# Expert stage: transposes and gathers as products with narrow array tiles

## The chip, the core and the metric

The kernel runs on one core of a Trainium2 chip. A core has five engines with their own instruction streams: TensorE (PE, matrix products out of SBUF into PSUM), VectorE (DVE), ScalarE (ACT), GpSimd (POOL) and SyncE (SP, which here issues the DMA transfers). The metric is the device time of one execution in microseconds. A product on PE is a weight load (LDWEIGHTS, the stationary operand) and a MATMUL that streams the moving operand past it. The array can be used whole (128 rows by 128 columns), or as column tiles of 64 or 32 columns, each with its own small product; in the profile's shapes "128*64" is a product on a tile of 128 rows and 64 columns.

## The reference

One inference step of a two-layer backbone for 128 context tokens and 128 latent tokens, 1024 channels, all in float32. Layer 0 mixes with a long convolution and RWKV-7 and has a dense SwiGLU; layer 1 mixes with gated DeltaNet and ends in a mixture of 8 experts, of which each token uses 2. The change lies in that last part:

```
def moe_swiglu(h, router, w_in, w_out):
    logits = (h @ router).astype(jnp.float32)
    top_val, top_idx = lax.top_k(logits, TOP_K)
    gates = jax.nn.softmax(top_val, -1)
    combine = jnp.einsum('blk,blke->ble', gates, jax.nn.one_hot(top_idx, N_EXP, ...))
    out = dense_swiglu(h, w_in[0], w_out[0]) * combine[..., 0:1]
    for e in range(1, N_EXP):
        out = out + dense_swiglu(h, w_in[e], w_out[e]) * combine[..., e:e + 1]
    return out
```

with `dense_swiglu(h, w_in, w_out)`: `gate, up = split(h @ w_in)`, then `(silu(gate) * up) @ w_out`, 1024 channels to 2 x 3584 and back.

## The kernel before

The work is one sequence of stages: modulation products and the even layer, the dense SwiGLU, the odd layer, the routing, and then the expert stage from line 1849 on (in the profile from 1036 us to 1915 us of the span), a final norm and the stores.

In the expert stage the 8 experts are sorted by their number of tokens and get a fixed number of slots in that order (`MAIN_CAPS`): 128 (WIDE), 64 (HALF), and then three times 96 (MID) and 64 (HALF). This stage is called the main pass; a second pass for tokens that don't fit is skipped here by a branch. For each expert, called q below, PE does:

- a gather (line 2071): it picks the expert's tokens out of `htok` by products with the 0/1 matrix `Psel`, two halves of 16 products in the code, into bank 5; ACT copies the result to `hA`;
- 7 steps of 512 hidden channels. A step is a gate product and an up product (`in_product`, line 2079), ACT and DVE make silu(gate) x up (`actb`), PE transposes that in blocks of 128x128 (line 2106) into bank 4, ACT copies it to `actT`, and PE multiplies it into the expert's output (`project`, line 2109);
- a transpose of the slot weights `Pw` (line 2141), and a scatter (line 2147) of the expert's output back to the tokens, four parts in the steps of the next expert.

The products are shaped by the slots. WIDE uses the whole array (lines 2086, 2121). HALF puts two products of 64 columns side by side (lines 2089, 2124). MID uses four tiles of 32 columns: three take 384 of the 512 weight columns (lines 2094, 2129), the fourth takes the remaining 128 for all three groups of tokens one after the other (lines 2097, 2132). Transposes, gathers and weight transposes use the whole array in every step, the scatter uses the whole width with as many rows as the expert has slots.

The order on PE in step i is written out by hand (line 2155): gate product of i, transposes of i-1, then one of: weight transposes (first step of an expert, for the expert before), scatter part (steps 1 to 4), gather half for the next expert (steps 5 and 6), then the up product of i and the output product of i-1. A transposed block is 128 columns of `actb`: there are 4 in a WIDE step, 3 in a MID step, 2 in a HALF step.

Weights come from HBM through a ring of 7 tiles of 2 MB (`load` in `sp_pass`): 3 tiles a step, 168 in the pass, one DMA each, all from SP in order. A load waits until PE has finished the product that used its slot 7 tiles before; a product waits until its tile has landed.

Of the kernel before, what the change touches and what calls it, by code (L numbers as in the profile page):

```python
# [14 lines left out]
P = 128  # L15
T = 128
# [10 lines left out]
NE = 8  # L27
# [120 lines left out]
def program(nc, A, O):  # L148
    ctx = ExitStack()
    with ctx:  # L150
# [28 lines left out]
        ps = [ctx.enter_context(nc.psum_tensor(f"bank{i}", [P, 512], F32)) for i in range(8)]  # L179
# [14 lines left out]
        def take(*shape, rows=P):  # L194

            n = 1
            for k in shape:
                n *= k
            assert floats[0] + n <= ARENA, (floats[0], n, ARENA)
            ap = arena[0:rows, floats[0]:floats[0] + n]  # L200
            floats[0] += n
            if len(shape) == 1:
                return ap
            names = "abcd"[:len(shape)]
            return ap.rearrange(f"p ({' '.join(names)}) -> p {' '.join(names)}", **{names[i]: shape[i] for i in range(len(shape))})
# [12 lines left out]
        def cc(name):  # L218
            g, o, k = CCOL[name]
            return cons[g][:, o:o + k]  # L220

        ident, ones, bones = cc("ident"), cc("ones"), cc("bones")
# [1626 lines left out]
        WIDE, MID, HALF = T, 3 * T // 4, T // 2  # L1849
# [6 lines left out]
        htok = take(NS, D)  # L1856
# [5 lines left out]
        Psel = take(NS, T)  # L1862
        Pw = take(NS, T)
# [147 lines left out]
        actb = take(2, 512)  # L2011
# [6 lines left out]
        KC = EFF // 512  # L2018
        STEPS = NE * KC
# [48 lines left out]

        def pe_pass(pe, m):

            def gather(q, half):
                c = m.caps[q]
                for j in range(4 * half, 4 * half + 4):
                    for s in range(NS):
                        mm = nc.tensor.matmul(ps[5][:, (j % 4) * T:(j % 4) * T + c], htok[:, s, j * P:(j + 1) * P], Psel[:, s, 0:c],  # L2075
                                              start=(s == 0), stop=(s == 1))
                mm.then_inc(m.gat, 1)

            def in_product(i, n, out):
                c, h = m.caps[i // KC], hA[:, (i // KC) % 2]  # L2080
                m.arrived(pe, n)
                w = m.tile(n).rearrange("p (j c) -> p j c", j=8)
                for j in range(DC):
                    start, stop = j == 0, j == DC - 1
                    if c == WIDE:
                        mm = nc.tensor.matmul(out[:], h[:, j, :], w[:, j, :], start=start, stop=stop)  # L2086
                    elif c == HALF:
                        for x in range(2):
                            mm = nc.tensor.matmul(out[HALF * x:HALF * x + HALF, 0:256], h[:, j, 0:HALF],  # L2089
                                                  w[:, j, 256 * x:256 * x + 256], start=start, stop=stop,  # L2090
                                                  tile_position=(0, HALF * x))
                    else:
                        for lo, hi in ((0, 32), (32, HALF), (HALF, MID)):
                            nc.tensor.matmul(out[lo:hi, 0:3 * P], h[:, j, lo:hi], w[:, j, 0:3 * P], start=start, stop=stop,  # L2094
                                             tile_position=(0, lo), skip_group_check=True)
                        for r in range(3):
                            mm = nc.tensor.matmul(out[MID:P, r * P:(r + 1) * P], h[:, j, 32 * r:32 * r + 32], w[:, j, 3 * P:4 * P],  # L2097
                                                  start=(start and r == 0), stop=stop, tile_position=(0, MID), skip_group_check=True)
                mm.then_inc(m.used, 1)

            def transposes(i):
                pe.wait_ge(m.act, m.base + i + 1)
                if i:
                    pe.wait_ge(m.aT, m.base + i)
                for f in range(m.width(i) // P):
                    mm = nc.tensor.transpose(ps[4][:, f * T:(f + 1) * T], actb[:, i % 2, f * P:(f + 1) * P], ident)  # L2106
                mm.then_inc(m.tr, 1)

            def project(i):
# [28 lines left out]
            def weights(q):  # L2138
                pe.wait_ge(m.Pw, m.base + q + 1)
                for s in range(NS):  # L2140
                    mm = nc.tensor.transpose(ps[5][:, s * T:(s + 1) * T], Pw[:, s, :], ident)
                mm.then_inc(m.Ct, 1)

            def scatter(q, b, bank):
                c = m.caps[q]
                for d in (2 * b, 2 * b + 1):
                    mm = nc.tensor.matmul(bank[:, (d % 2) * TT:(d % 2 + 1) * TT], ye[0:c, d * P:(d + 1) * P], Cw[0:c, :],  # L2147
                                          start=True, stop=True)
                mm.then_inc(m.sc, 1)

            pe.wait_ge(m.P, m.base + 1)
            gather(0, 0)
            pe.wait_ge(m.hA, m.base + 1)
            gather(0, 1)
            for i in range(STEPS):
                q, k = divmod(i, KC)
                if k == 0:
                    pe.wait_ge(m.hA, m.base + 2 * q + 2)
                if i >= 2:
                    pe.wait_ge(m.act, m.base + i - 1)  # L2160
                in_product(i, gate_at(i), ps[2 * (i % 2)])
                if i:
                    transposes(i - 1)
                if k == 0 and q:
                    weights(q - 1)
                if 1 <= k <= 4 and q:
                    if k == 1:
                        pe.wait_ge(m.C, m.base + q)
                        pe.wait_ge(m.ye, m.base + q)
                    else:  # L2170
                        pe.wait_ge(m.acc, m.base + 4 * (q - 1) + k - 1)
                    scatter(q - 1, k - 1, ps[5])
                if k >= 5 and q < NE - 1:
                    if k == 5:
                        pe.wait_ge(m.P, m.base + q + 2)
                        if q:
                            pe.wait_ge(m.acc, m.base + 4 * q)
                    else:
                        pe.wait_ge(m.hA, m.base + 2 * q + 3)
                    gather(q + 1, k - 5)  # L2180
                if i == STEPS - 1:
                    pe.wait_ge(m.acc, m.base + 4 * q)
                    weights(q)
                in_product(i, up_at(i), ps[2 * (i % 2) + 1])
                if i:
                    project(i - 1)
            transposes(STEPS - 1)
            project(STEPS - 1)
            pe.wait_ge(m.act, m.base + STEPS)
# [125 lines left out]
        with nc.Block() as block:  # L2315
# [25 lines left out]
            @block.tensor  # L2341
            def _(pe):
                with pe.If(more(pe) > 0):
                    pe_pass(pe, rest)
                    pe.wait_ge(rest.acc, rest.base + 4 * NE)
                pe_pass(pe, main)
                n4.pe(pe, ps[0])
# [142 lines left out]
```

## Time and profile before

| what | value |
|---|---|
| median of 3 runs | 1940.58 us (1939.35 to 1944.2) |
| the profiled execution's own time | 1933.93 us |
| its span, first to last instruction | 1932.2 us |
| PE busy | 1777.2 us (92%), 18321 MATMULs |
| granted PE clock, mean of the span | 0.962 |
| DMA queue of the weights (q1) | 489.90 MB, 61.7% of 16 engines' span |
| instruction fetch (q8) | 146 packets, 2.39 MB |

The profile gives busy time by engine, a picture of the span in slices, the chain of work that ended last (followed back from the last instruction), and groups of instructions by line. Times are in us from the start of the span. A float32 product in the code stands in the trace as two LDWEIGHTS and two MATMULs, a transpose as one of each. MATMULs overlap, so the pace of a group is its length in the chain over its count, not the mean duration of one.

### The profile page before, as it was taken

Reading aid. Unit: us, or ns where it says so; the run is one execution under the profiler, and the core shown is the slowest. Engines: PE = TensorE matmul, PEld = TensorE weight load, DVE = VectorE, ACT = ScalarE, POOL = GpSimd, SP = SyncE. Lnnn points to the kernel's source line nnn. Section 1 sums busy time; section 2 is a strip of 40 time slices with the busy share of each in tenths; the row PEclk is TensorE's granted clock in tenths of the full one; section 3 lists DMA queues with packets and bytes.
Section 4 is the critical chain, followed back from the end, with each engine's and each line's share of the span. In section 5 each row is a group of like instructions: output and inputs, shape, how many; then the busy total and the mean of one; then the engine's idle time right before and its main releaser. Section 6 shows DMA issues by size and latency. Waiting matters only on the chain. (4 is left out here: it accounts for less than half of the span.)

```text
span 1932.2 us, 40334 instructions
## 1 busy us (share of the span) xinstructions
PE 1777.2 (92%) x18321; PEld 1399.3 (72%) x18321; DVE 533.4 (28%) x1222; ACT 294.5 (15%) x638; POOL 72.3 (4%) x109
## 2 busy tenths in 40 slices
PE   6996888899999898788887999999999999999995
PEld 3884777778888687677775444579966897589853
DVE  5436667530000347266633000100000000000003
ACT  1112333110000143323211000010010001000101
POOL 0002222000000000000000000000000000000000
PEclk9998999999999899888896999999999999999998
DMA  9809542224342432000004987999999999999993
GB/s 390 332 25 428 204 177 89 99 87 174 131 174 88 180 136 88 7 13 13 13 6 186 428 338 302 419 426 426 420 421 426 426 424 421 428 425 426 408 428 166
DMA packets 37133, 492.54 MB, mean 255 GB/s; under 512 B 4380, under 2 KB 4541, under 8 KB 7453
## 3 DMA queue, kind: packets, MB, share of 16 engines
q1 hardware_dynamic: 36956, 489.90, 61.7%
q8 instruction: 146, 2.39, 0.5%
q14 instruction: 31, 0.25, 0.0%
HBM read 487.53 MB, written 2.36 MB: 254 GB/s over the span
## 5 line engine op out<-in xcount | busy, mean ns | idle before, releaser
L2097 PE MATMUL bank<-ring,arena 128*32 128x128 f32 x2016 | 227.6, 273 | 0.0
L2094 PE MATMUL bank<-ring,arena 128*32 128x384 f32 x2016 | 224.8, 487 | 1.8 <-DMA ring<-in_experts 1.8
L2097 PEld LDWEIGHTS bank<-ring,arena 128*32 128x32 f32 x2016 | 217.9, 110 | 0.0
L2089 PE MATMUL bank<-ring,arena 128*64 128x256 f32 x1792 | 204.8, 381 | 2.7 <-DMA ring<-in_experts 2.7
L2089 PEld LDWEIGHTS bank<-ring,arena 128*64 128x64 f32 x1792 | 126.2, 137 | 80.2 <-issue 22.5
L2291 DVE TENSOR_TENSOR arena<-bank,arena 128x256 f32<-128x256 f32 (+2 forms) x56 | 28.5, 508 | 545.1 <-PE bank L2097 155.1
L1374 PE MATMUL bank<-arena,ring 128*128 128x256 f32 x704 | 155.3, 382 | 4.0 <-DVE arena L321 3.8
L1374 PEld LDWEIGHTS bank<-arena,ring 128*128 128x128 f32 x704 | 133.9, 191 | 24.5 <-issue 4.1
L2247 ACT ACTIVATE arena<-bank 128x256 f32<-128x256 f32 (+2 forms) x56 | 25.3, 452 | 697.4 <-PE bank L2097 293.6
L1495 PE MATMUL bank<-arena,ring 128*128 128x256 f32 x512 | 115.6, 388 | 6.4 <-DVE arena L321 3.8
L1495 PEld LDWEIGHTS bank<-arena,ring 128*128 128x128 f32 x512 | 98.6, 194 | 24.8 <-issue 5.8
L2132 PE MATMUL bank<-ring,arena 128*32 128x128 f32 x1008 | 113.5, 273 | 0.0
L2129 PE MATMUL bank<-ring,arena 128*32 128x384 f32 x1008 | 112.1, 486 | 0.0
L2132 PEld LDWEIGHTS bank<-ring,arena 128*32 128x32 f32 x1008 | 109.8, 110 | 0.0
L2124 PE MATMUL bank<-ring,arena 128*64 128x512 f32 x448 | 101.2, 593 | 3.9 <-DMA ring<-in_experts 3.9
L2086 PE MATMUL bank<-ring,arena 128*128 128x512 f32 x224 | 98.3, 593 | 1.5 <-DMA ring<-in_experts 1.5
L2265 DVE TENSOR_TENSOR arena<-arena,bank 128x512 f32<-128x512 f32 x32 | 22.0, 688 | 274.4 <-PE bank L2147 274.4
L583 PE MATMUL bank<-arena,ring 128*128 128x256 f32 (+1 forms) x416 | 92.1, 385 | 5.0 <-DVE arena L297 5.0
L583 PEld LDWEIGHTS bank<-arena,ring 128*128 128x128 f32 (+1 forms) x416 | 80.0, 193 | 16.9 <-issue 5.2
L2094 PEld LDWEIGHTS bank<-ring,arena 128*32 128x32 f32 x2016 | 80.6, 109 | 11.7 <-issue 11.3
L2086 PEld LDWEIGHTS bank<-ring,arena 128*128 128x128 f32 x224 | 42.0, 190 | 51.9 <-issue 50.2
L1385 PE MATMUL bank<-arena,ring 128*128 128x256 f32 x352 | 77.0, 379 | 0.0
(393 smaller groups left out, 2210.2 us busy)
## 6 DMA issues: line engine op xcount, KB each, us to landing
ring<-in_experts SPq DMA_DIRECT2D x168, 2048.0 KB, 20.5
ring<-in_stream SPq DMA_DIRECT2D x61, 2048.0 KB, 11.9
xT<-in_xT SPq DMA_DIRECT2D x1, 1024.0 KB, 7.4
arena<-in_s0gd SPq DMA_DIRECT2D x4, 256.0 KB, 3.4
out_sgd<-arena SPq DMA_DIRECT2D x4, 256.0 KB, 2.5
out_y<-arena SPq DMA_DIRECT2D x4, 256.0 KB, 2.5
arena<-in_masks SPq DMA_DIRECT2D x1, 832.0 KB, 7.1
arena<-in_hfw SPq DMA_DIRECT2D x1, 544.0 KB
```

Of the source, the lines that this page charges most:

```text
L583: mm = nc.tensor.matmul(ps[m % 4][0:rows, 0:TT], tile_in(n)[:, j, f * P:f * P + rows], hT[:, j, :], start=(j == 0), stop=(j == DC - 1))
L1374: mm = nc.tensor.matmul(ps[4 + m % 4][:, half * TT:(half + 1) * TT], w[:, j, half * 256 + f:half * 256 + f + P], hT[:, j, :], start=(j == ...
L1385: mm = nc.tensor.matmul(ps[d // 2][:, (d % 2) * TT:(d % 2 + 1) * TT], tile_out(tile)[:, f % 4, d * P:(d + 1) * P], act4[:, k % 2, f % 4, : ...
L1495: mm = nc.tensor.matmul(ps[m % 4][:, 0:TT], tile_in(n)[:, j, f * P:(f + 1) * P], hT[:, j, :], start=(j == 0), stop=(j == DC - 1))
L2086: mm = nc.tensor.matmul(out[:], h[:, j, :], w[:, j, :], start=start, stop=stop)
L2089: mm = nc.tensor.matmul(out[HALF * x:HALF * x + HALF, 0:256], h[:, j, 0:HALF], w[:, j, 256 * x:256 * x + 256], start=start, stop=stop, til ...
L2094: nc.tensor.matmul(out[lo:hi, 0:3 * P], h[:, j, lo:hi], w[:, j, 0:3 * P], start=start, stop=stop, tile_position=(0, lo), skip_group_check= ...
L2097: mm = nc.tensor.matmul(out[MID:P, r * P:(r + 1) * P], h[:, j, 32 * r:32 * r + 32], w[:, j, 3 * P:4 * P], start=(start and r == 0), stop=s ...
L2124: mm = nc.tensor.matmul(ps[6][HALF * h:HALF * h + HALF, :], aT[:, f % 2, o:o + HALF], w[:, f, 512 * h:512 * h + 512], start=start, stop=st ...
L2129: nc.tensor.matmul(ps[6 + h][lo:hi, 0:3 * P], aT[:, f, lo:hi], w[:, f, o:o + 3 * P], start=start, stop=stop, tile_position=(0, lo), skip_g ...
L2132: mm = nc.tensor.matmul(ps[6 + h][MID:P, r * P:(r + 1) * P], aT[:, f, 32 * r:32 * r + 32], w[:, f, o + 3 * P:o + 4 * P], start=(start and ...
L2291: V.tensor_tensor(actb[:, i % 2, 0:n], ps[2 * (i % 2) + 1][:, 0:n], sgl[:, i % 2, 0:n], ALU.mult).then_inc(m.act, 1)
```

## The change

A helper `strands` writes one product of the code as 128/w products of w columns each, one on each column tile of the array, where w is the width of the products of the expert that PE is working on then: 128 in WIDE, 64 in HALF, 32 in MID. The two transposes (of `actb` and of `Pw`) become such products with the unit matrix `ident` as the moving operand, and the gather's products are cut the same way. WIDE is included: there a transpose becomes one whole product with `ident`. The scatter is left as it is, and so are the order of the steps, the waits and the loads.

```diff
--- before.py
+++ after.py
@@ -2068,12 +2068,21 @@
 
         def pe_pass(pe, m):
 
-            def gather(q, half):
+            STRAND = {WIDE: P, HALF: 64, MID: 32}
+
+            def strands(out, left, right, q, start=True, stop=True):
+                w = STRAND[m.caps[q]]
+                for x in range(0, P, w):
+                    mm = nc.tensor.matmul(out[x:x + w], left[:, x:x + w], right, start=start, stop=stop,
+                                          tile_position=(0, x), skip_group_check=True)
+                return mm
+
+            def gather(q, half, during):
                 c = m.caps[q]
                 for j in range(4 * half, 4 * half + 4):
                     for s in range(NS):
-                        mm = nc.tensor.matmul(ps[5][:, (j % 4) * T:(j % 4) * T + c], htok[:, s, j * P:(j + 1) * P], Psel[:, s, 0:c],
-                                              start=(s == 0), stop=(s == 1))
+                        mm = strands(ps[5][:, (j % 4) * T:(j % 4) * T + c], htok[:, s, j * P:(j + 1) * P], Psel[:, s, 0:c], during,
+                                     start=(s == 0), stop=(s == 1))
                 mm.then_inc(m.gat, 1)
 
             def in_product(i, n, out):
@@ -2103,7 +2112,7 @@
                 if i:
                     pe.wait_ge(m.aT, m.base + i)
                 for f in range(m.width(i) // P):
-                    mm = nc.tensor.transpose(ps[4][:, f * T:(f + 1) * T], actb[:, i % 2, f * P:(f + 1) * P], ident)
+                    mm = strands(ps[4][:, f * T:(f + 1) * T], actb[:, i % 2, f * P:(f + 1) * P], ident, min(i + 1, STEPS - 1) // KC)
                 mm.then_inc(m.tr, 1)
 
             def project(i):
@@ -2138,7 +2147,7 @@
             def weights(q):
                 pe.wait_ge(m.Pw, m.base + q + 1)
                 for s in range(NS):
-                    mm = nc.tensor.transpose(ps[5][:, s * T:(s + 1) * T], Pw[:, s, :], ident)
+                    mm = strands(ps[5][:, s * T:(s + 1) * T], Pw[:, s, :], ident, min(q + 1, NE - 1))
                 mm.then_inc(m.Ct, 1)
 
             def scatter(q, b, bank):
@@ -2149,9 +2158,9 @@
                 mm.then_inc(m.sc, 1)
 
             pe.wait_ge(m.P, m.base + 1)
-            gather(0, 0)
+            gather(0, 0, 0)
             pe.wait_ge(m.hA, m.base + 1)
-            gather(0, 1)
+            gather(0, 1, 0)
             for i in range(STEPS):
                 q, k = divmod(i, KC)
                 if k == 0:
@@ -2177,7 +2186,7 @@
                             pe.wait_ge(m.acc, m.base + 4 * q)
                     else:
                         pe.wait_ge(m.hA, m.base + 2 * q + 3)
-                    gather(q + 1, k - 5)
+                    gather(q + 1, k - 5, q)
                 if i == STEPS - 1:
                     pe.wait_ge(m.acc, m.base + 4 * q)
                     weights(q)
```

PE's order around the first HALF expert's first two steps, as the program issues it (a row is line, operation, out<-in, shape of the output, number in the code). Before, L2089 and L2124 are HALF products, L2121 WIDE output products, L2106 and L2141 transposes, L2147 the scatter:

```order
L2121 MATMUL bank<-ring,arena 128x512 x8
L2089 MATMUL bank<-ring,arena 64x256 x16
L2106 MATMUL bank<-con,arena 128x128 x4
L2141 MATMUL bank<-con,arena 128x128 x2
L2089 MATMUL bank<-ring,arena 64x256 x16
L2121 MATMUL bank<-ring,arena 128x512 x8
L2089 MATMUL bank<-ring,arena 64x256 x16
L2106 MATMUL bank<-con,arena 128x128 x2
L2147 MATMUL bank<-arena 128x256 x2
L2089 MATMUL bank<-ring,arena 64x256 x16
```

and of the changed kernel, where L2098, L2133 and L2130 are those products, L2156 the scatter, and L2076 the product inside `strands`:

```order
L2130 MATMUL bank<-ring,arena 128x512 x8
L2098 MATMUL bank<-ring,arena 64x256 x16
L2076 MATMUL bank<-con,arena 64x128 x12
L2098 MATMUL bank<-ring,arena 64x256 x16
L2130 MATMUL bank<-ring,arena 128x512 x8
L2098 MATMUL bank<-ring,arena 64x256 x16
L2076 MATMUL bank<-con,arena 64x128 x4
L2156 MATMUL bank<-arena 128x256 x2
L2098 MATMUL bank<-ring,arena 64x256 x16
```

The four transposes of a WIDE step and the two of the weights became 12 products of 64 columns, and the two transposes of a HALF step 4; they stand at the same place.

The same around a gather in a MID step; before, L2094 and L2097 are the MID products and L2075 is the gather:

```order
L2094 MATMUL bank<-ring,arena 32x384 x3
L2097 MATMUL bank<-ring,arena 32x128 x3
L2106 MATMUL bank<-con,arena 128x128 x3
L2075 MATMUL bank<-arena 128x64 x8
L2094 MATMUL bank<-ring,arena 32x384 x3
L2097 MATMUL bank<-ring,arena 32x128 x3
```

and after, where L2103 and L2106 are the MID products:

```order
L2103 MATMUL bank<-ring,arena 32x384 x3
L2106 MATMUL bank<-ring,arena 32x128 x3
L2076 MATMUL bank<-con,arena 32x128 x12
L2076 MATMUL bank<-arena 32x64 x32
L2103 MATMUL bank<-ring,arena 32x384 x3
L2106 MATMUL bank<-ring,arena 32x128 x3
```

Three transposes became 12 products of 32 columns, and the gather's 8 products of 128 columns became 32 of 32 columns.

## Rows read from the trace of the kernel before

**Rows 1.** Windows: length; PE, PEld, DVE, ACT, POOL busy (count); clock; DMA share; GB/s.

```profile
1050.00:1115.00 65.00, 65.00 (x162) 29.39 (x161) 2.46 (x5) 3.86 (x7) 0.00 (x0) 1.00 1.01 429
1120.00:1192.00 72.00, 72.00 (x203) 34.27 (x203) 2.58 (x5) 4.03 (x8) 0.00 (x0) 1.00 0.80 294
1207.00:1905.00 698.00, 689.77 (x8645) 535.14 (x8645) 47.99 (x100) 61.63 (x169) 0.00 (x0) 1.00 1.00 420
1390.00:1406.00 16.00, 16.00 (x238) 13.71 (x232) 0.56 (x1) 1.22 (x4) 0.00 (x0) 1.00 0.98 392
1486.00:1695.00 209.00, 206.87 (x2711) 165.85 (x2711) 14.19 (x30) 18.47 (x51) 0.00 (x0) 1.00 1.01 425
1695.00:1905.00 210.00, 204.29 (x2683) 162.71 (x2683) 13.79 (x28) 18.15 (x51) 0.00 (x0) 1.00 0.98 412
```

**Rows 2.** DMA in 1125 to 1207 us: issues, KB, median us to landing.

```profile
ring<-in_experts SPq DMA_DIRECT2D x12, 2048.0 KB, 7.7
```

**Rows 3.** DMA in 1207 to 1905 us: instruction fetch, and the tiles' issues.

```profile
q8 instruction: 68, 1.11, 0.6%
...
ring<-in_experts SPq DMA_DIRECT2D x139, 2048.0 KB, 21.7
```

**Rows 4.** Chain of waits, WIDE expert: start us, length us, what.

```profile
1068.94 0.44 PE bank L2106 x4
...
1153.54 1.73 PE bank L2075 x16
```

**Rows 5.** Chain of waits, from WIDE into the first HALF expert.

```profile
1195.49 0.59 PE bank L2106 x4
1196.08 0.22 PE bank L2141 x2
1196.30 3.60 PE bank L2089 x32
1199.90 7.06 PE bank L2121 x16
1206.97 3.60 PE bank L2089 x32
```

**Rows 6.** Chain of waits, a HALF step with a scatter, and a gather.

```profile
1242.30 3.45 PE bank L2089 x32
1245.75 0.37 PE bank L2106 x2
1246.12 0.87 PE bank L2147 x4
1246.98 3.60 PE bank L2089 x32
...
1257.85 1.76 PE bank L2075 x16
```

**Rows 7.** Chain of waits, MID: transposes with a scatter, and before a gather.

```profile
1316.96 0.48 PE bank L2106 x3
1317.44 1.06 PE bank L2147 x4
...
1785.22 0.48 PE bank L2106 x3
```

**Rows 8.** Chain of waits: loads from issue to landing, at three HALF ends.

```profile
1460.57 25.51 DMA ring<-in_experts
...
1667.58 27.56 DMA ring<-in_experts
...
1876.64 28.43 DMA ring<-in_experts
```

**Rows 9.** PE's waits, 1395 to 1500 us: line, releaser, us, times, longest.

```profile
PE bank L2094 <- DMA ring<-in_experts: 0.6, 1, 0.6
```

**Rows 10.** PE instructions by form: busy us, mean ns.

```profile
L2106 PE MATMUL bank<-con,arena 128*128 128x128 f32 x147 | 28.0, 292 | 0.0
```

**Rows 11.** Timeline of PE, modulation products: start us, length us, what.

```profile
197.90 2.61 PE L376 MATMUL bank<-ring,silc 128*32 128x128 f32 x88
```

## The prediction

> **What bounds the kernel now.** I read the windows of the expert stage first. From 1120 to 1192 us, in the WIDE expert, PE is busy all the time and the DMA engines only 0.80 of it: the ring is full, and each load waits for PE. From 1207 to 1905 us the DMA share is 1.00 at 420 GB/s [rows 1]. The DMA view says the same: a tile lands 7.7 us after its issue up to 1207 [rows 2], and 21.7 us after it from there on [rows 3], so that several loads always stand in the queue. So the stage has two parts. Up to about 1207 the end moves with PE. From there it moves with the DMA: 139 loads stand in a row, and PE is late only where the ring is full.
>
> How far PE is from the bound there: after the second HALF expert (1486 us) PE waits 0.6 us for a tile [rows 9], in the next pair of MID and HALF 209.00 - 206.87 = 2.1 us, and in the last pair 210.00 - 204.29 = 5.7 us [rows 1]. The waits grow, so PE is the faster of the two over a pair, by about 2 us. The chain of waits names loads at just these three HALF ends [rows 8]. Their landings are 1460.57 + 25.51 = 1486.08, 1695.14 and 1905.07, 42 tiles, so a pair takes the loads 209.06 and 209.93 us. The one place where the ring still throttles is where MID goes over into HALF: 392 GB/s in 1390 to 1406, against 425 in 1486 to 1695 [rows 1], which is 0.077 x 16 = 1.2 us. The granted clock is 1.00 in all these windows.
>
> **The change on PE.** A transpose is one MATMUL now: 147 in the trace [rows 10] for 7 x 4 + 28 x 2 + 21 x 3 blocks in the code. Four take 0.44 us [rows 4], 0.11 each. A product with the unit matrix is two MATMULs, as every float32 product is (the order has 16 products in a HALF gate, the chain 32 [rows 6]). At the same size (128 columns of weights) the gather's run takes 1.73 / 16 = 0.108 each [rows 4], and narrow tiles run side by side: 88 MATMULs on 32-column tiles with 128 moving columns take 2.61 us in all, about 0.03 each [rows 11], or 0.11 per tile. So a block costs 0.22 instead of 0.11, whatever the width of its strands.
>
> Against this stand the changes of tile width. In HALF two transposes take 0.37 and not 0.22, so going in costs 0.15; and the next product takes 3.60 where it takes 3.45 without a change before it [rows 6], so coming out costs 0.15. In MID three take 0.48 instead of 0.33 [rows 7]: again 0.15. The return there I take as in HALF. In WIDE nothing changes width, and nothing is saved.
>
> - **WIDE:** six steps with transposes, each 8 x 0.108 - 0.44 = +0.43. Sum +2.6 us. The gathers here keep their shape.
> - **The first HALF step:** four blocks of WIDE and two of the weights take 0.59 + 0.22 now, and 0.15 for coming out: 0.96 [rows 5]. After: 24 MATMULs on two tiles, 12 x 0.11 = 1.31, with no change of width. +0.35 us. If the two tiles did not run at once it were 2.6, +1.7. The 3.45 us for 32 MATMULs of 256 columns [rows 6], 0.108 each where one alone at 0.11 per 128 columns needs 0.22, say that they do.
> - **HALF, other steps:** with a scatter (four of them) the change of width stays, since the scatter is wide: +0.22 each. With a gather (two): +0.22 for the transposes, -0.30 for the width, and the gather between its present 1.76 and, with two tiles at once and 96 moving columns, 16 x 0.11 x 96 / 128 = 1.32: -0.08 to -0.52 each. The later first steps (three blocks and two): 5 x 0.11 - 0.30 = +0.25. An expert: +0.1 to +1.0.
> - **MID:** with a scatter +0.33 for three blocks; of two changes of width, before the transposes and before a scatter of 64 rows (1.06 against 0.87 [rows 6, 7]), one goes: +0.18, four times. With a gather: +0.33 - 0.30, and the gather, now 1.73 like WIDE's, between 64 x 0.03 = 1.9, the fastest sustained pace of a row [rows 11], and 16 x 0.11 x 64 / 128 = 0.9 with four tiles at once: +0.2 to -0.8, twice. First step: 0.44 - 0.30 = +0.14. An expert: +1.3 to -0.7.
>
> A pair of MID and HALF changes by -0.6 to +2.3 us, and I take the middle, +0.8, as the rows price the scatter steps and not the faster gathers. This lies beside the loads: PE has about 2 us to spare in a pair. If that cover is gone, or if PE's lateness at the full ring of a MID end is handed to the loads, up to 1 us for each of three MIDs counts: +3; a gain there counts likewise, down to -2. I take 0.
>
> **The change at the DMA engines.** More MATMULs are more instructions to fetch, over the same engines as the tiles. From 1207 to 1905 the fetch is 68 packets and 1.11 MB [rows 3] for 8645 MATMULs [rows 1]: 128 bytes for each with its weight load. The change adds 1047 MATMULs after 1207 (each MID expert +250: 140 for `actb`, 14 for the weights, 96 for the gather; the HALFs +68, +83, +83 and, with no gather, +63), so 0.13 MB or 8 packets. A packet takes 0.6% x 16 x 698 / 68 = 1.0 us of an engine. Spread evenly that is 0.5 us; all on the engine that lands each tile last it is 8 us. Between them: at the 429 GB/s of 1050 to 1115 us, where PE has 162 MATMULs in 65 us [rows 1], a pair's 42 tiles were 42 x 2.097 MB / 429 = 205.3 us. They take 209.06 and 209.93 [rows 8], 3.8 and 4.6 more, with about 2700 MATMULs [rows 1]. If all of that is the fetch, it is 1.56 ns per MATMUL, and 1047 cost 1.6 us. I take this one, as the only value that comes from the pace of the last engine. Nothing covers it: the loads are the path.
>
> **Sum:** 2.6 + 0.35 + 0 + 1.6 = +4.6 us. DVE, ACT and SP keep their work; ACT's copy after a transpose starts up to 0.43 us later, and an up product, 3.60 us even in HALF [rows 5], stands before the output product that needs it. After the last landing, 1905.07, PE has only the last output product and the scatter, both unchanged. The profiled execution took 1933.93 us, and would take 1938.5; it stands 6.65 below the median of the runs, 1940.58, to which I add the same: 1945.2 us, +0.24%. A measurement of this kernel can tell about 0.3% from no change, 5.8 us; this is below it.
>
> The Trainium skill, "TensorE: Matmul & The Clock Gate", section "Terms", says that the transpose mode is 4 times faster for float32, which speaks against this change: by that rule a block would cost 0.44 us as a product, and the time were that of rival 2. The trace does not agree: it has 0.11 us for a transpose and two MATMULs of 0.108 for a product [rows 4].
>
> **The rivals.**
> 1. Slower: the loads take the added work worse than by the mean. The eight fetches fall on the engine that lands last, and the MIDs, late by the scatter steps, hold back the loads at a full ring. The place is the MID ends and the queue from 1207 on; 2.95 with 4 to 8 for the fetch and up to 3 for the MIDs, of which I take +9: 1949.6 us. For it: the pair's excess over full rate, 3.8 and 4.6 us, is more than an even spread gives (68 packets in 698 us are 20 in 209, 20 x 1.0 / 16 = 1.3). Against it: PE's waits grow from pair to pair. It decides once half of the eight fetches fall on that engine (2.95 + 4 > 5.8).
> 2. A product with the unit matrix costs four transposes, 0.44 us a block: WIDE 6 x 4 x 0.33 = 7.9, the first HALF step 6 x 0.44 - 0.96 = 1.7, with the fetch 11.2: 1951.8 us. Against it stands the gather's run at the same size.
> 3. Less than forecast: the gathers run at their fast end, PE's gain at the MID ends lets loads start earlier, and the fetch spreads evenly: 2.95 + 0.5 - 2 = +1.4, 1942 us. For it: 392 GB/s at the MID end shows that PE is not quite out of it. Against it: what is gained there must be seen by the last engine, whose landings keep an even pace [rows 8].
> 4. Faster: the saved changes of width count in all HALF and MID steps, and a product costs no more than a transpose. Two changes of 0.15 in the 19 gather and first steps and one in the 12 MID scatter steps are 7.5 us: 1933.1. For it, the rows of 0.37 and 3.60; against it, those of 0.44 and 1.73, and the DMA share of 1.00, beside which none of it would show.
>
> **How the numbers follow.** Forecast 0.57, rivals in their order 0.22, 0.04, 0.12 and 0.05. The forecast's own range is 1942.5 to 1948; the runs of before spread from 1939.35 to 1944.2, so that a fifth of its chance is read as slower (0.12) and the rest as no change (0.45). Rival 1 gives 0.18 slower and 0.04 same, rival 2 0.04 slower, rival 3 0.12 same, rival 4 0.05 faster. Together: faster 0.05, same 0.61, slower 0.34. The range from 1939.5 to 1952 holds the forecast, rival 3 within the spread of runs, and most of rival 1.
>
> **What would show it.** In the chain, a WIDE step's transposes as x8 with 0.87 us; the first HALF expert's product at 1206.97 about 2.9 us later; the HALF and MID gather steps without the longer product behind them; 76 or so fetch packets after 1207; the DMA share still 1.00, and PE still waiting at the HALF ends. I am wrong if the last pairs' landings lie more than 1 us wider apart than 209.9, if PE no longer waits for tiles in the last HALF expert, or if a block in WIDE takes other than 0.22 us.

## The result, and the profile of the changed kernel

The changed kernel takes 1946.09 us (median of 22 runs, 1941.04 to 1950.21), the kernel before, beside it, 1941.54 (22 runs, 1935.06 to 1946.76). The ratio is 1.0024, 95% interval [1.0016, 1.0031]: 4.7 us slower by the ratio, from 3.1 to 6.0 (the two medians lie 4.55 apart). The forecast was +4.6.

The windows of the expert stage come first: length, busy time of PE, PEld, DVE, ACT and POOL with their counts, granted clock, DMA share, GB/s. The stage begins some 6 us later in this execution, so the stretches are those of [rows 1], moved.

```profile
1050.00:1115.00 65.00, 62.66 (x169) 29.79 (x170) 2.46 (x5) 5.37 (x8) 0.00 (x0) 1.00 1.00 428
1130.00:1200.00 70.00, 70.00 (x206) 34.49 (x205) 2.58 (x5) 4.37 (x8) 0.00 (x0) 1.00 0.77 283
1216.00:1917.00 701.00, 693.05 (x9695) 545.67 (x9696) 47.97 (x100) 63.10 (x169) 0.00 (x0) 1.00 1.00 419
1400.00:1416.00 16.00, 15.51 (x242) 13.59 (x236) 0.56 (x1) 1.21 (x4) 0.00 (x0) 1.00 0.95 369
1496.00:1706.00 210.00, 207.59 (x3046) 168.82 (x3044) 14.18 (x30) 18.87 (x51) 0.00 (x0) 1.00 1.00 424
1706.00:1917.00 211.00, 206.33 (x2998) 166.84 (x3000) 13.79 (x28) 18.66 (x51) 0.00 (x0) 1.00 0.98 410
```

The picture is that of before: PE bounds the WIDE expert (DMA share 0.77), the loads bound the rest (1.00, 419 GB/s). After the crossing from the WIDE into the first HALF expert 1050 MATMULs more stand in the trace (9695 against 8645). The end of a MID moves the ring at 369 GB/s instead of 392.

The DMA view from 1214 to 1918 us gives packets, MB and share of the queue that fetches instructions, and the tiles' issues with their median time to landing:

```profile
q8 instruction: 76, 1.25, 0.7%
...
ring<-in_experts SPq DMA_DIRECT2D x139, 2048.0 KB, 20.8
```

Eight packets more than in [rows 3], as forecast; the loads still stand in a row.

The chain of waits, from a WIDE step through the crossing into the first HALF expert (start, length, what; L2076 is the product in strands, L2095 and L2130 are WIDE's products, L2098 and L2133 HALF's, L2156 the scatter):

```profile
1075.23 0.89 PE bank L2076 x8
...
1096.73 0.89 PE bank L2076 x8
...
1204.51 1.31 PE bank L2076 x24
1205.81 3.45 PE bank L2098 x32
1209.27 7.06 PE bank L2130 x16
1216.33 3.60 PE bank L2098 x32
1219.94 0.44 PE bank L2076 x8
1220.37 1.06 PE bank L2156 x4
1221.43 3.60 PE bank L2098 x32
...
1267.89 1.76 PE bank L2076 x40
1269.65 3.45 PE bank L2098 x32
```

A WIDE step's transposes are x8 and 0.89 us where [rows 4] have 0.44: the step from one to the next is 21.49 us, 21.04 before. The transposes at the crossing take 1.31, and no longer product stands behind it (3.45), against 0.96 in [rows 5]. The product that was at 1206.97, 166.70 us after the first load's issue, is at 1216.33, 169.82 after it: +3.12. In HALF a scatter step has 0.44 + 1.06 where [rows 6] have 0.37 + 0.87: +0.26. In a gather step transposes and gather together take 1.76, as long as the gather alone did, and the product behind is the short one: 12.10 us from step to step, 12.62 before.

The same chain in a MID expert, and the two loads on it at HALF ends (L2103 is MID's product on narrow tiles):

```profile
1361.80 0.66 PE bank L2076 x18
1362.45 1.06 PE bank L2156 x4
...
1379.36 1.38 PE bank L2076 x69
...
1385.24 0.36 issue
...
1403.93 0.49 issue
...
1679.86 26.28 DMA ring<-in_experts
...
1890.05 26.65 DMA ring<-in_experts
```

A MID scatter step has 0.66 where [rows 7] have 0.48: +0.18. The gather step's burst (transposes and gather, 88 MATMULs) is done in about 1.6 us where 0.48 and 1.73 stood. But PE then waits for "issue" in the middle of the next product, and the gain is gone: the two gather steps of a MID take 34.8 to 35.0 us, 34.50 before. The loads land at 1706.14 and 1916.70, 210.56 us apart, where [rows 8] have 209.93.

PE's waits in 1216 to 1920 us (line, releaser: us in total, times, longest):

```profile
PE bank L2133 <- DMA ring<-in_experts: 2.9, 3, 1.3
PE bank L2098 <- DMA ring<-in_experts: 1.5, 2, 1.2
PE bank L2103 <- DMA ring<-in_experts: 1.2, 1, 1.2
PE bank L2103 <- issue: 1.2, 3, 0.5
PE bank L2076 <- issue: 0.5, 2, 0.3
PE bank L2106 <- issue: 0.4, 1, 0.4
```

PE still waits for tiles at the HALF ends, 5.6 us in all. The last three lines are new. A wait is counted from the end of the last product's record, so a stop of PE is longer than its wait: from the start of one MATMUL to the start of the next, the waits of 0.36 and 0.49 us in the chain above are gaps of 0.85 and 0.76.

To compare kernels I use the landing records of all 168 tiles: tile 41 is the last of the first HALF expert, tiles 83, 125 and 167 end the three pairs of MID and HALF. Before, the pairs take 210.06 + 209.06 + 209.93 = 629.05 us; after, 210.50 + 210.56 + 210.56 = 631.62, +2.57. Tile 41 lands 2.8 us later after the first tile, the last one 5.3. The profiled execution is 13.66 us longer (1947.59 against 1933.93): 5.3 are these, 6.2 lie before the first load of the stage, and 1.9 behind the last landing. The last two don't come from the change: in the experiments the first load is issued anywhere between 1043.4 and 1050.6 us, and the tail is anything from 27.0 to 29.4, whatever was edited.

### The profile page after: what moved, and what is told of

It is laid out like the page before. It is cut to its first block and busy times, and to the rows that moved or that the text cites. A ratio compares the mean times of both kernels' runs of the same rounds, so it can differ in the third digit from the quotient of the medians.

```text
span 1945.7 us, 42512 instructions
## 1 busy us (share of the span) xinstructions
PE 1791.1 (92%) x19410; PEld 1420.9 (73%) x19410; DVE 532.4 (27%) x1222; ACT 296.8 (15%) x638; POOL 72.2 (4%) x109
## 5 line engine op out<-in xcount | busy, mean ns | idle before, releaser
L2103 PE MATMUL bank<-ring,arena 128*32 128x384 f32 x2016 | 227.3, 487 | 2.4 <-DMA ring<-in_experts 1.2
L2106 PE MATMUL bank<-ring,arena 128*32 128x128 f32 x2016 | 228.5, 273 | 0.5 <-issue 0.4
L2106 PEld LDWEIGHTS bank<-ring,arena 128*32 128x32 f32 x2016 | 217.9, 110 | 2.0 <-issue 2.0
L2098 PE MATMUL bank<-ring,arena 128*64 128x256 f32 x1792 | 204.3, 381 | 1.5 <-DMA ring<-in_experts 1.5
L2098 PEld LDWEIGHTS bank<-ring,arena 128*64 128x64 f32 x1792 | 127.1, 137 | 76.9 <-issue 21.1
L2141 PE MATMUL bank<-ring,arena 128*32 128x128 f32 x1008 | 113.5, 273 | 0.0
L2141 PEld LDWEIGHTS bank<-ring,arena 128*32 128x32 f32 x1008 | 109.8, 110 | 0.0
L2133 PE MATMUL bank<-ring,arena 128*64 128x512 f32 x448 | 101.2, 593 | 3.0 <-DMA ring<-in_experts 2.9
L2095 PE MATMUL bank<-ring,arena 128*128 128x512 f32 x224 | 98.3, 593 | 1.8 <-DMA ring<-in_experts 1.8
L2103 PEld LDWEIGHTS bank<-ring,arena 128*32 128x32 f32 x2016 | 81.6, 109 | 12.6 <-issue 12.6
L2095 PEld LDWEIGHTS bank<-ring,arena 128*128 128x128 f32 x224 | 42.0, 190 | 52.2 <-issue 52.2
```

Source lines behind the costliest of these rows:

```text
L2133: mm = nc.tensor.matmul(ps[6][HALF * h:HALF * h + HALF, :], aT[:, f % 2, o:o + HALF], w[:, f, 512 * h:512 * h + 512], start=start, stop=st ...
L2141: mm = nc.tensor.matmul(ps[6 + h][MID:P, r * P:(r + 1) * P], aT[:, f, 32 * r:32 * r + 32], w[:, f, o + 3 * P:o + 4 * P], start=(start and ...
```

## The experiments

The theory: 3 us come from PE ahead of the crossing, PE's later steps are hidden beside the loads, and the rest is instruction fetch on the loads' engines. The rival: the rest is PE's lateness, handed to the loads.

**e1_wide_back.** The changed kernel, with the six WIDE steps' transposes as before:

```
+ if i + 1 < KC:
+     mm = nc.tensor.transpose(ps[4][:, f * T:(f + 1) * T], actb[...], ident)
+ else:
      mm = strands(ps[4][:, f * T:(f + 1) * T], actb[...], ident, ...)
```

> The changed kernel with the transposes of the WIDE expert's first six steps put back (24 blocks); everything else as changed. My theory, a PE-bound stretch up to the first HALF steps and a DMA-bound one behind it: the first HALF expert's output product of WIDE is back by 2.6 us, and the last tile lands 2.6 us sooner than in the changed kernel, so +2.0 us to the kernel before (ratio 1.001). Rival, all of the 4.6 us is paid in the HALF and MID experts (fetch, or PE late at a full ring): the time stays at +4.6 (1.0024).

1944.53 us against 1940.99, ratio 1.0015 [1.0004, 1.0026]: +2.9 us, from 0.8 to 5.0, which holds both theories. The landings are sharper: tile 29 is back near its place (169.7 us after the first tile; 168.9 before, 171.2 changed), the pairs stay long (631.81). So WIDE gives its part back, and the other part remains.

**e2_wide_alone.** The kernel before, with strands in WIDE and the first HALF step only (that is, products with the unit matrix where the changed kernel has them up to step 6).

> The kernel before with nothing but the WIDE expert's steps and the first HALF step changed (28 blocks of WIDE and the first two of the weights as products); no gather and no later transpose. My theory: +2.95 us (ratio 1.0015), seen whole in the landing of the last tile, with the landings of later pairs 209 to 210 us apart as before. Rival, the loads catch up behind WIDE: 0.

1944.01 us, ratio 1.0014 [1.0002, 1.0027]: +2.7 us, from 0.4 to 5.2, with the pairs at 629.15 as before. The interval is wide, but the landings say the same. Tile 29 lands 168.6 to 169.9 us after the first tile in ten executions of kernels that leave WIDE's steps as they were; in the three with products there (the changed kernel, this one and e8 below) it lands after 171.2 to 172.1. So the 2.95 of the sum are borne out, and they stay out of the pairs.

**e3_mid_late.** The kernel before, with the transposes of one step in each MID repeated six times more, 2 us of PE time:

```
+ late = (i + 1) % KC == 4 and ... and m.caps[(i + 1) // KC] == MID
+ for f in [g for r in range(7 if late else 1) for g in range(m.width(i) // P)]:
```

> The kernel before with PE made late in each of the three MID experts: the three transposes of one step (the fifth) are issued seven times instead of once, 18 MATMULs or 2.0 us each time, with the same result. Hardly an instruction more to fetch. My theory, MID and HALF lie beside the loads: under +1 us in all (the first MID end has the least room), PE's waits for tiles at the HALF ends shrink by up to 2 us. Rival, PE's lateness at a full ring is handed to the loads: +6.0 us (1.003).

1940.47 us, ratio 0.9993 [0.9981, 1.0006], pairs 629.42. Six us of PE time cost 0.4 at the landings, while PE's waits for tiles shrink from 8.4 to 3.7 us. Lateness in MID is hidden.

**e5_half_late.** The same in HALF, ten times in all.

> The kernel before with PE made late in each of the four HALF experts: the two transposes of one step (the fifth) are issued ten times instead of once, 18 MATMULs or 2.0 us each time, same result. My theory: the tiles land as before (three pairs in 629 us, as 210.06 + 209.06 + 209.93 in the kernel before), PE's waits for tiles shrink. Rival, PE's lateness counts: up to +8 us.

One run, 1940.59 us (before 1942.1), pairs 629.48; PE's waits for tiles shrink from 8.4 to 1.8 us. They are the cover.

**e4_fetch.** The kernel before, with 5000 small memsets on GpSimd, to load the fetch without touching PE.

> The kernel before with 5000 one-element memsets on GpSimd beside the expert stage, which writes nothing that is read: instructions to fetch, no work for PE. If they are fetched over the same engines as the others, 64 bytes each are 0.32 MB or 20 packets more. My theory, fetches delay the tiles at 1.56 ns per 128 bytes: +3.9 us (1.002), seen in the distance of the landings. Rival, the fetch spreads over 16 engines: 20 x 1.0 / 16 = +1.2 us. If PE's lateness is the whole of it: 0.

1943.95 us, ratio 1.0006 [0.9993, 1.0019]. It tells nothing of the fetch beside the loads. GpSimd's instructions come over another queue (69 packets where it had 31), and the memsets ran too early: from 1044.7 to 1234.4 us, most of it in the WIDE expert, where PE and not the loads is the bound. Their packets came as they ran, and only 12 stand between 1207 and 1905 us instead of 7.

**e6_split_out and e7_split_in.** The kernel before, with MID's output products, or its gate and up products, of 384 columns cut into three of 128, each tile's three in a row:

```
- nc.tensor.matmul(out[lo:hi, 0:3 * P], h[:, j, lo:hi], w[:, j, 0:3 * P], ...)
+ for y in range(0, 3 * P, P):
+     nc.tensor.matmul(out[lo:hi, y:y + P], h[:, j, lo:hi], w[:, j, y:y + P], ...)
```

> The kernel before with the MID experts' output products cut: each product of 384 moving columns becomes three of 128, on the same tile with the same weights. The same columns stream on each tile (the fourth tile's three products of 128 set the pace before and after), but 2016 MATMULs more are fetched. My theory, fetch delays the tiles: at 1.56 ns per MATMUL (prediction) the three pairs take 3.1 us longer than before's 629 us, at the 2.6 ns that the changed kernel shows (631.6 us for 1000 more) 5.3 us. Rival, the fetch costs nothing at the tiles: 629 us.

> The kernel before with the MID experts' gate and up products cut in the same way: 4032 MATMULs more to fetch, the same columns on each tile. My theory: three pairs +6.3 us at 1.56 ns, +10.7 us at 2.6 ns, and the time with them (ratio 1.003 to 1.0055), PE still waiting for tiles at the HALF ends. Rival, fetch is spread or hidden: three pairs within 1 us of 629, ratio 1.000. A third outcome: PE itself runs out of instructions, which would show as waits of PE for nothing but the issue, and the pairs longer with no waits for tiles.

1996.1 us (one run) and 2056.2, ratio 1.0591 [1.0571, 1.0611]: far more than any of the sums. Of the third outcome the longer pairs came (744.6 us in e7) and the waits for tiles went away, but not its sign: PE waits for the issue only once, 0.4 us. The window of a MID in e7 (columns as above):

```profile
1560.00:1640.00 80.00, 80.00 (x1666) 76.81 (x1664) 4.42 (x7) 4.13 (x12) 0.00 (x0) 1.00 0.82 323
```

PE is busy all the time and the DMA share falls to 0.82: PE became the bound. One eighth of a product was 12 MATMULs in some 0.66 us and is now 24, which take some 41 ns each, 0.99 us. A tile has 6 of these 24, which take 0.66 us at 0.11 each, so with three pieces for one tile in a row the four tiles no longer run all at once. The experiment says nothing on the fetch; together with e9 below it shows that the order of the pieces over the tiles counts.

**e8_mid_gather_wide.** The changed kernel, with MID's gathers wide as before.

> The changed kernel with only the gathers issued in MID experts (six halves) put back to the full width: 288 MATMULs fewer, two changes of width more in each of the six steps. In the changed kernel such a pair of steps takes 34.9 us, as long as before (34.5), though the gather itself became faster. If the burst of 88 small products is what costs the products behind it (PE waits for its own issue there), the two steps go to 0.33 for the transposes above before: 35.2 us, without issue waits. If something else lengthens them, they keep 34.9 with the waits, or grow by the 0.8 us that the wide gather takes more.

One run, 1947.26 us; pairs 630.06, with 81 fetch packets in the stage, over both queues, where the changed kernel has 83. Its two gather steps take 35.50 us, longer than the changed kernel's 34.9, and no wait for issue is left. In e1, where the code of MID is the changed kernel's, they take 35.5 to 35.8, so the waits differ from one execution to the next. PE is as late here as in e1 and later than in the changed kernel, and the pairs are shorter than in either (631.81 and 631.62): PE's lateness isn't what lengthens them, as far as one execution can say.

**e9_rotate_in and e10_rotate_all.** e7's cut with the pieces issued in turn over the four tiles, then the output products too:

```
+ for r in range(3):
+     for lo, hi in ((0, 32), (32, HALF), (HALF, MID)):
+         nc.tensor.matmul(out[lo:hi, r * P:(r + 1) * P], h[:, j, lo:hi], w[:, j, r * P:(r + 1) * P], ...)
      mm = nc.tensor.matmul(out[MID:P, r * P:(r + 1) * P], ...)
```

> The kernel before, with MID's gate and up products of 384 columns cut into three of 128 as in e7_split_in, but issued in turn over the four column tiles (the first 128 columns on tiles 0, 1, 2 and 3, then the second, then the third), so that four tiles run at once. Same numbers, 4032 MATMULs more after 1207 us (3 MIDs x 14 products x 96). My theory, the fetch of instructions beside the loads at 1.56 ns per MATMUL: 106 fetch packets where before has 75, the three pairs of MID and HALF +6.3 us together, the time +6.3 us (ratio 1.0032). If what the changed kernel lost in the pairs (2.4 us for 1047 MATMULs, 2.3 ns each) is all fetch: +9.3 us (1.0048). Rival, the fetch costs the loads nothing and what the changed kernel lost there is PE's: within 1 us of before, as PE's pace stays at some 27 ns per MATMUL. If PE itself becomes the bound, as in e7_split_in, the waits for tiles at the HALF ends go away and a MID product takes well over 5.3 us.

> As e9_rotate_in, and MID's output products cut and issued in turn in the same way: 6048 MATMULs more than before after 1207 us. A dose half as large again: by the fetch at 1.56 ns per MATMUL +9.4 us (1.0049), at 2.3 ns +13.9 us (1.0072), some 121 fetch packets; by the rival within 1 us of before. The pairs of MID and HALF should grow by 1.5 times what e9_rotate_in's grow if the fetch is the cause; they need not if it is PE.

2036.16 us, ratio 1.051 [1.049, 1.0531], and 2100.64, ratio 1.0818 [1.079, 1.0846]; pairs 719.4 and 778.5. The sums missed by far. What came is the case named last, PE as the bound, but for a new reason. PE's waits in e9, 1216 to 1980 us:

```profile
PE bank L2095 <- issue: 38.5, 27, 2.8
PE bank L2097 <- issue: 13.5, 8, 3.1
PE bank L2129 <- issue: 5.2, 5, 2.3
PE bank L2132 <- issue: 3.7, 3, 1.5
PE bank L2075 <- issue: 1.6, 1, 1.6
```

62.5 us of waits, none for a tile. The chain of waits at one of them (L2095 and L2097 are the cut products):

```profile
1554.85 0.10 PE bank L2095 x3
1554.95 0.01 PE bank L2097
1554.96 2.25 issue
1557.21 0.31 PE bank L2095 x3
1557.52 0.01 PE bank L2097
```

Four MATMULs in 0.11 us, 27 ns each, then a stop of 2.25 us. The DMA view of 1554.5 to 1556 us has one packet of the fetch:

```profile
q8 instruction: 1, 0.02, 4.4%
```

By the packets' records it moves from 1554.81 to 1555.87, and PE goes on 1.34 us later. It is so at all nine stops of over 0.25 us between 1545 and 1640 us: each ends 1.3 to 1.6 us after the end of a fetch packet, and six of them stand 127 or 128 MATMULs behind the one before. A packet of 16 KB holds 128 MATMULs at 128 bytes each with its weight load. So PE ran out of instructions. The 16 packets that start between 1545 and 1640 us come 5.9 us apart on the mean (13 of the 15 distances between 5.3 and 8.0, two near 3.5), which is 46 ns per MATMUL, and the cut products want one in 27. Of the 90 us that the pairs grew, the waits are 62.5; the granted clock, 0.96 in 1560 to 1640 where it was 1.00, may be another part, and how the rest is made up I did not resolve.

**e11_half_alone.** Strands in the HALF experts only.

> The change in the HALF experts alone; WIDE and MID keep their transposes and wide gathers. 297 MATMULs more after 1207 us. My theory: the first HALF step +0.35 us, the fetch 297 x 1.56 ns = +0.5, the gather steps 0.5 us shorter each and hidden beside the loads: +0.8 us (1.0004), pairs of MID and HALF together +0.5. Rival, the shorter gather steps at the HALF ends let loads start earlier: 6 x 0.5 = 3 us less at most, -2 us (0.9990). If MID is what cost the changed kernel its 2.4 us in the pairs, this one's pairs stay at 629 to 629.5 us.

1941.2 us, ratio 1.0003 [0.9993, 1.0014], pairs 629.58. As by the theory; the shorter gather steps at the HALF ends gain nothing.

**e12_half_cut.** The dose that e9 missed, at a pace that the fetch can follow: HALF's products cut into pieces of 128 columns, in turn over the two tiles.

```
- for x in range(2):
-     mm = nc.tensor.matmul(out[HALF * x:HALF * x + HALF, 0:256], ...)
+ for y in range(0, 256, P):
+     for x in range(2):
+         mm = nc.tensor.matmul(out[HALF * x:HALF * x + HALF, y:y + P], ...)
```

> The kernel before, with all products of the HALF experts cut into pieces of 128 columns, issued in turn over the two column tiles. Same numbers, 784 MATMULs more per HALF expert, 2352 in the three pairs of MID and HALF, 3136 in all after 1207 us; each then takes some 54 ns (3.45 us for 64), as the MATMULs of MID's products do already, so that PE should not run out of instructions as it did in e9_rotate_in at 27 ns. About 100 fetch packets where before has 75. My theory, the fetch over the DMA engines holds up the loads by 1.56 ns per MATMUL: pairs 629.05 + 3.7 = 632.7 us, the time +4.9 us (ratio 1.0025); if what the changed kernel lost in the pairs is all fetch (2.4 ns): 634.7 us and +7.5 us (1.0039). Rival, the fetch packets cost the loads nothing and what the changed kernel lost is PE's alone: pairs at 629 to 629.5 us, the time within 1 us of before. If PE runs out of instructions here too, waits for issue stand at the HALF products.

1946.39 us against 1940.22, ratio 1.003 [1.0018, 1.0041]; pairs 634.01. The fetch from 1214 to 1918 us, and PE's waits in 1207 to 1950 (L2127, L2095 and L2090 are products of HALF, MID and HALF):

```profile
q8 instruction: 92, 1.51, 0.9%
```

```profile
PE bank L2127 <- DMA ring<-in_experts: 4.7, 4, 2.0
...
PE bank L2095 <- DMA ring<-in_experts: 2.6, 3, 1.2
PE bank L2090 <- DMA ring<-in_experts: 2.5, 3, 1.0
```

The chain of waits, a HALF step and two loads:

```profile
1224.34 3.49 PE bank L2090 x64
1227.83 0.37 PE bank L2107 x2
1228.20 0.87 PE bank L2151 x4
1229.07 3.65 PE bank L2090 x64
1232.71 3.49 PE bank L2127 x64
...
1467.46 25.65 DMA ring<-in_experts
...
1886.66 28.97 DMA ring<-in_experts
```

64 MATMULs take 3.49 us where 32 took 3.45, and a step grows by 0.14 us only. PE waits for tiles 9.8 us, more than before (8.4), and not for issue: it isn't what holds the pairs back. Two pairs lie between the landings of 1493.11 and 1915.63: 422.52 us, where [rows 8] have 418.99. That is 3.53 us for 1568 MATMULs; the three pairs give 4.96 for 2352, 2.1 ns each, or 0.27 us per packet. The time gives 5.8 us for 3136, 1.9 ns, from 1.1 to 2.5. So MATMULs added beside the loads cost the loads, though PE has time for them.

That it is the fetch of their instructions, and not the weight loads that come with them and read SBUF while the tiles are written there, is likely but not settled. If the tiles' own packets were slowed, they would show it. Between the landings of tiles 41 and 167 they take 552.3 ns each on the mean, where the kernel before and e2 to e5 have 551.0 to 551.8. Against the kernel before, summed and shared over 16 engines, that is 1.4 us of the 4.96; the 19 fetch packets more, at 1.05 us, are 1.2, and the remaining 2.4 are time in which engines stand idle. In the changed kernel the three parts of the 2.57 are 1.4, 0.5 and 0.7.

## Why the prediction was right

- **WIDE and the crossing.** Forecast 2.95, measured 3.12 in the chain, and +2.7 us [0.4, 5.2] by e2. A block of 0.22 was read from the gather's run [rows 4] and stands in the trace as 8 MATMULs in 0.89. The reading had some luck: the gather of that row streams 64 columns per MATMUL, the HALF expert's slots, and the product with the unit matrix 128. Both take 0.11 us, which that row alone didn't show. The Trainium skill, "TensorE: Matmul & The Clock Gate", section "Terms", gives the transpose mode a factor of 4 for float32; the trace has 0.44 against 0.89 for the same blocks, a factor of 2, and the measurement decides.
- **HALF and MID hidden.** I took 0 for a pair that PE does between 0.6 us faster and 2.3 slower. e3 (2 us more in each MID, 0.4 at the landings of all three), e5 and e8 show the cover. The rival's 3 us for late MIDs did not come. That the ring falls to 369 GB/s at the first MID's end is no sign of them: e3 and e5 fall to 370 and 380 there, with pairs of 629.4 and 629.5.
- **The steps in detail.** HALF's scatter step grew by 0.26 (forecast 0.22), the gather step shrank by 0.52, the fast end of my range; MID's scatter step grew by 0.18 as forecast. MID's gather steps were forecast between +0.2 and -0.8 and came at about +0.2 each (0.5 to 0.7 in e1): the burst is about as fast as four tiles at once can be, and what it gains PE gives back waiting for its next 128 MATMULs. In the changed kernel the two waits on the chain above end 1.3 and 1.5 us after a fetch packet's end, as in e9. I had no such row, and it cost nothing only because PE was hidden there.
- **The fetch.** Its place was right, beside the loads and with nothing to cover it, but this term was mis-sized: 1.56 ns per MATMUL, 1.6 us, where the pairs grew by 2.57. About 979 of the added MATMULs lie in these pairs, so 2.6 ns each; e12 measures 2.1 (2.25 by the two pairs of the chain). I had read the price from the pairs' excess over an undisturbed full rate, which assumes that the loads are otherwise as fast as in the WIDE expert; the two readings are 1.3 to 1.7 times mine. e8 (691 MATMULs, +1.0) and e11 (229, +0.5) lie around the same line, from one execution each, with some 0.4 us between kernels that should be equal (629.05 to 629.48). How a packet of 1.1 us on one of 16 engines holds up the landings by 0.27 and not by 0.07 isn't shown; that the engine which lands last takes more than its share would do it, and the idle time in e12 would fit that.
- **The sum.** 3.12 and 2.57 are 5.7, the last landing is 5.3 later, and the ratio gives 4.7 [3.1, 6.0]. The forecast of 4.6 lies in that interval, with a fetch term that was 1 us low. That it lies within 0.1 us of 4.7 is luck: the parts add up to 5.3 to 5.7. The prediction also took a change of 0.3% as the least that can be told from none; with 22 runs of each kernel this one, of 0.24%, stands clear of the noise.
- **The signs named.** x8 with 0.87 (0.89), the product 2.9 later (3.12), 76 packets (76), the DMA share of 1.00 and waits at the HALF ends came as said; the last pair is 0.6 us wider than 209.93, under the 1 us named.

Rival 2 fell with the 0.89, rival 4 with the loads still in a row, rival 1 by the interval's high end of 6.0 us and by e3. Rival 3 is out by the interval's low end of 3.1.

## What to carry to other kernels

Where transfers bound a stage, count the instructions that a change adds on the engine as well as its time: some 2 ns for each MATMUL beside a full DMA queue is little for one edit, but it is not hidden as PE's time is. Cutting products into smaller ones is nearly free for PE only while a MATMUL takes longer than its instructions take to come, here 46 ns on the mean (e9) with 54 still safe (e12), and while neighbours in the order lie on different tiles. A lateness on an engine with waits is cheap to test: repeat a small instruction until the waits are used up.

## What had not been expected of the hardware

- PE can run out of instructions. Beside a full queue of loads, 128 MATMULs came every 5.9 us on the mean; products at 27 ns stood still for up to 3.1 us (e9), those of before at 55 ns, and e12's at 54, did not.
- Four 32-column tiles run all at once when the products are issued in turn over them, 27 ns per MATMUL (e9); with three products in a row on one tile it is 41 ns (e7).
- After MATMULs on 64-column tiles the scatter takes 1.06 us where it takes 0.87 after whole-array transposes: the change of width that goes in front of the transposes comes back behind them.
- GpSimd's 5000 memsets added no packet to the queue that fetches PE's instructions, 146 before and after; their own came over another, 69 where it had 31 (e4).
